# State-space loop of a two-layer trunk: gated pieces of one channel block over both pairs, decays in SBUF, two PSUM banks for input products, parameter tables loaded in two parts

## The chip, the cores and the metric

One core of a Trainium2 chip runs the whole kernel. The metric is the device time of one execution in microseconds; shown is the median of three. The engines are PE (TensorE), DVE (VectorE), ACT (ScalarE), POOL (GpSimd) and SP, which here only issues transfers.

## The reference, cut to what matters

A trunk of two layers over 256 frames of 2048 channels. Layer 0 mixes with a gated linear recurrence and windowed attention, layer 1 with a grouped state-space model (128 groups of 16 channels, 64 complex states each) and a gated layer; each layer has a squared-ReLU MLP of hidden size 8192. The change touches the mixer of layer 1:

```
h = rmsnorm(x, mix_norm_o[j])
# s5_grouped
lam_bar = exp(lam * step);  bu = einsum('blgh,gph->blgp', u, b_bar)
_, h = lax.associative_scan(_linear_combine, (broadcast(lam_bar), bu), axis=1)
y = real(einsum('blgp,ghp->blgh', h, c)) + d_skip * u
# gated layer
g = gelu(y) @ w_glu[j]
val, gate = split(g, 2, axis=-1)
x = x + val * sigmoid(gate)
```

All of it is float32. A product with a weight is done as two matmuls: the rounded weight `Wh` times the operand and its remainder side by side (512 columns), and the weight's remainder `Wl` times the operand (256 columns).

## The kernel before, in words

**Weights.** A weight matrix is taken in pairs of 128 output channels (256 columns); a pair is four units of 512 rows. SP loads a unit to `raw`, ACT rounds it to `Wh` (L1055), DVE writes the remainder `Wl = raw - Wh` (L1418), PE runs 16 matmuls for each unit. ACT (L1060) and DVE (L1489) evict a finished pair from its two PSUM banks in `ps`; the second pair behind needs these banks, so `pair` on PE waits for `pair_read` of the pair two before it.

**The state-space loop.** The 2048 channels are 16 blocks `c`. The frames are handled four at a time, so 64 steps are left to scan; four groups of steps with real and imaginary part make 512 columns. Per block:

- POOL `s5_input` (L2195): scales the input rows `us` by the norm's factor. Five are done ahead of the loop (`INPUTS_AHEAD`), then one in each step of the loop.
- PE `s5_in`: 32 matmuls of 64x64x64 with the table's rows into `v_bank`: `px[:,0]` for even blocks, `ps[:,1]` for odd ones below block `V_ALONE = 13`, `px[:,0]` for all from 13 on.
- DVE `s5_rotate` (L1792, L1793): two multiplies with the table's cos and sin, from PSUM to `ab`.
- POOL `s5_turned` (L2202): `zb`, their difference.
- ACT `s5_decay` (L1332): fills the PSUM bank `px[:,1]` with the block's decays, behind the scan before it.
- DVE `s5_scan` (L1801): `tensor_tensor_scan` over `px[:,1]` and `zb` into `px[:,3]`, then two multiplies with cos and sin to `pp` (L1806, L1807).
- POOL `s5_unturned` (L2208): adds the two parts of `pp`.
- PE `s5_out`: 48 matmuls with the table's output columns into `px[:,2]`.
- ACT `s5_gelu` (L1341) to `yb`; SP stores it to `y_d` and loads it turned to `yt` (L564); ACT `s5_high` (L1346) and POOL `s5_low` (L2213) write it to the operand `A2`.

DVE's order is rotate(c+1), scan(c), `pp`(c). PE's step c is `s5_in(c+1)`, `s5_out(c-2)`, and from c = 10 a piece of the gated layer. POOL's step c is turned(c), unturned(c-1), an input, and from c = 6 to 13 low(c-6); the lows 8 to 15 come behind the loop.

**Tables.** Each block has one of 1 MB in DRAM (`par_d`): columns `S_IN:S_OUT` are the rows for `s5_in`, then output columns, direct part, cos, sin. Six slots in SBUF hold them. SP loads table c+6 whole, once `s5_out(c)` has been done and after the store of block c; five of the six first ones are loaded during the last MLP phase of layer 0.

**The gated layer beside the loop.** Its first two pairs are eight units `u` (s, h = divmod(u, 2): quarter s of the rows, pair h). `glu_piece(n)` is one half (t) of one unit: eight matmuls, for which all four channel blocks of quarter s must be there. Pieces 0 to 5 stand in steps 10 to 15, piece 6 ahead of `s5_out(15)`, pieces 7 to 15 behind it. Piece 3 waits for the rotation of block 11, because the loop uses a bank of `ps`.

**Behind the loop.** SP loads the next pair's weights (`load_third`) behind the last turned block. ACT and DVE split two units of them, then evict pair `P_GLU`, split the third, evict the pair behind it, split the fourth. PE goes on with pair `P_GLU + 2`.

## Time and profile before

| | |
|---|---|
| median of three executions | 2044.24 us (2044.02 to 2044.94) |
| the profiled execution | 2049.94 us |
| its span | 2048.2 us |
| PE busy | 1999.4 us, 98% |
| DVE busy | 1341.9 us, 66% |
| ACT busy | 941.2 us, 46% |
| POOL busy | 710.3 us, 35% |
| mean granted TensorE clock | 0.996 |

The busy times are sums over the span, and matmuls overlap, so PE's is close to the whole. The loop with the state-space model lies between about 1068 and 1142 us. A row of a timeline has the start, the duration, the engine, the line, the operation with its output and inputs, the count, and in brackets how long the engine stood before it and what released it.

### The profile page before, as it was taken

How to read it: one execution, taken by the hardware profiler on the slowest of the kernel's cores; microseconds unless marked ns; L12 is line 12 of the kernel's file. 1: busy time of each engine (PE TensorE's matmuls, PEld its weight loads, DVE VectorE, ACT ScalarE, POOL GpSimd, SP SyncE). 2: the span in 40 equal slices, each digit the busy share in tenths (PEclk: the TensorE clock that was granted, in tenths of full speed). 3: DMA queues.
4: the chain of work that ended last, by engine and by line, in shares of the span. 5: the costliest groups of instructions: out<-in, count | busy, mean ns of one | idle time of the engine just before them, and what ended most of it. 6: DMA issues, size and time to landing. Idle time of an engine off the chain costs nothing.

```text
span 2048.2 us, 35555 instructions
## 1 busy us (share of the span) xinstructions
PE 1999.4 (98%) x12950; PEld 1723.3 (84%) x12950; DVE 1341.9 (66%) x1470; ACT 941.2 (46%) x1244; POOL 710.3 (35%) x910
## 2 busy tenths in 40 slices
PE   8989999999999999999997999999999999999998
PEld 7778888888888888888876888888888888888887
DVE  6886888755765576566669666676566556656653
ACT  6446654444444444444553444444444444444443
POOL 3582369978677777440348311000000000000000
PEclk9999999999999999999999999999999999999999
DMA  7544567666666666676887555655556555656563
GB/s 219 177 118 134 171 182 211 197 224 203 203 201 216 204 197 226 196 261 194 290 255 261 174 184 171 198 185 186 186 182 188 190 185 175 194 185 186 180 194 128
DMA packets 374595, 399.89 MB, mean 195 GB/s; under 512 B 23152, under 2 KB 367488, under 8 KB 370400
## 3 DMA queue, kind: packets, MB, share of 16 engines
q1 hardware_dynamic: 366912, 371.77, 57.9%
q0 software_dynamic: 5216, 24.52, 4.1%
q10 hardware_dynamic: 2368, 2.24, 0.3%
q8 instruction: 67, 1.10, 0.2%
q14 instruction: 32, 0.26, 0.0%
HBM read 371.87 MB, written 25.17 MB: 194 GB/s over the span
## 4 chain that ended last, share of the span: by engine, by line
PE 88%; DVE 5%; ACT 3%; POOL 2%; issue 1%; DMA 1%; ACTq 0%; DVEq 0%; POOLq 0%; SPq 0%
PE ps L654 55%; PE ps L656 27%; DVE Wl L1418 1%; PE px L877 1%; ACT Wh L1055 1%; POOL pp L2208 1%; PE ps L990 1%; POOL zb L2202 1%; PE px L839 1%; DMA raw<-in_w_up_dram 0%; ACT pb L1135 0%; PE ps L625 0%; PE ps L839 0%; PE px L790 0%; POOL us L2195 0%
## 5 line engine op out<-in xcount | busy, mean ns | idle before, releaser
L654 PE MATMUL ps<-A,Wh 128*128 128x512 f32 x5024 | 1766.1, 400 | 4.5 <-issue 2.4
L656 PE MATMUL ps<-A,Wl 128*128 128x256 f32 x5024 | 1359.5, 281 | 0.0
L1418 DVE TENSOR_TENSOR Wl<-raw,Wh 128x1024 fp32r<-128x1024 f32 x660 | 840.7, 1286 | 563.4 <-ACT Wh L1055 556.9
L654 PEld LDWEIGHTS ps<-A,Wh 128*128 128x128 f32 x5024 | 926.1, 188 | 213.8 <-issue 6.0
L1055 ACT ACTIVATE Wh<-raw 128x1024 fp32r<-128x1024 f32 x660 | 689.9, 1058 | 738.7 <-PE ps L656 463.1
L656 PEld LDWEIGHTS ps<-A,Wl 128*128 128x128 f32 x5024 | 948.4, 189 | 28.9
L1249 ACT ACTIVATE A<-cross 128x512 f32 (+1 forms) x64 | 40.5, 633 | 207.2 <-DVE cross L1737 207.2
L1903 POOL TENSOR_TENSOR sq<-xT 128x512 f32<-128x512 f32 (+1 forms) x23 | 32.2, 1399 | 285.6 <-DVE xT L1823 152.7
L1489 DVE TENSOR_TENSOR cross<-ps,cross 128x512 f32<-128x512 f32 x161 | 110.0, 683 | 16.9 <-ACT cross L1060 16.6
L1060 ACT ACTIVATE cross<-ps 128x512 f32<-128x512 f32 x163 | 94.8, 581 | 11.5 <-PE ps L654 10.0
L1740 DVE TENSOR_TENSOR A<-cross,A 128x512 f32 (+1 forms) x64 | 47.5, 743 | 57.5 <-ACT A L1249 57.5
L1499 DVE TENSOR_TENSOR xT<-xT,cross 128x512 f32<-128x512 f32 (+1 forms) x72 | 53.9, 748 | 7.2 <-DVE cross L1489 5.9
L2125 POOL TENSOR_TENSOR t<-cti,lamp 128x256 f32<-128x256 f32 x16 | 19.9, 1244 | 96.7 <-ACT cti L1287 96.7
L1737 DVE SCALAR_TENSOR_TENSOR cross<-cross 128x512 f32<-128x512 f32 x64 | 49.3, 771 | 2.2
L1735 DVE TENSOR_TENSOR cross<-cross,rs 128x512 f32<-128x512 f32 x64 | 47.4, 741 | 2.2
L1506 DVE SCALAR_TENSOR_TENSOR A<-xT,pcol,A 128x256 fp32r<-128x256 f32 (+1 forms) x32 | 30.5, 1000 | 12.1 <-ACT A L1376 11.2
L1904 POOL TENSOR_TENSOR ss<-ss,sq 128x512 f32<-128x512 f32 x23 | 33.1, 1440 | 1.8
L2030 POOL TENSOR_TENSOR stg<-t 128x32 f32<-128x32 f32 (+2 forms) x48 | 32.1, 669 | 3.8
L2028 POOL TENSOR_TENSOR t<-stg 128x32 f32<-128x32 f32 (+2 forms) x48 | 27.3, 569 | 3.8
L2026 POOL TENSOR_TENSOR t<-stg 128x32 f32<-128x32 f32 (+2 forms) x48 | 25.3, 527 | 3.8
L990 PE MATMUL ps<-A,Wh 128*128 128x512 f32 x64 | 24.1, 417 | 1.9 <-POOL A L2213 1.1
L2029 POOL TENSOR_TENSOR t<-stg 128x32 f32<-128x32 f32 (+2 forms) x48 | 24.2, 504 | 3.8
(345 smaller groups left out, 1377.8 us busy)
## 6 DMA issues: line engine op xcount, KB each, us to landing
raw<-in_w_up_dram SPq DMA_DIRECT2D x256, 512.0 KB, 4.0
raw<-in_w_down_dram SPq DMA_DIRECT2D x256, 512.0 KB, 4.1
raw<-in_w_glu_dram SPq DMA_DIRECT2D x64, 512.0 KB, 4.3
raw<-in_w_in_e_dram SPq DMA_DIRECT2D x52, 512.0 KB, 3.9
raw<-in_w_out_e_dram SPq DMA_DIRECT2D x32, 512.0 KB, 3.4
s_params<-stg POOLq DMA_DIRECT2D x16, 1024.0 KB, 5.4
slot<-s_params SPq DMA_DIRECT2D x12, 1024.0 KB, 6.6
xin<-in_x_dram SPq DMA_DIRECT2D x4, 512.0 KB, 8.0
```

The source lines that it names most:

```text
L654: wide = lambda: mm(ps[:, b + t, :], Wh[:, s, c, cols], A[:, k, :], start=(n == 0), stop=(n == KC - 1))
L656: half = lambda: mm(ps[:, b + t, 0:L], Wl[:, s, c, cols], A[:, k, 0:L], start=False, stop=False)
L990: wide = lambda: mm(ps[:, 2 * d + t, :], Wh[:, u % NU, c, cols], A2[:, k, :], start=(k == 0), stop=(k == KC - 1))
L1055: fn(Wh[:, s], raw[:, s], ACT.Copy).then_inc(hi_split, 1)
L1060: fn(cross[:, d], banks[:, :, L:2 * L], ACT.Copy).then_inc(crossed, 1)
L1249: hi.inc(fn(A2[:, bass.ds(j * 2, 2), 0:L], cross[:, c], ACT.Copy))
L1418: tt(Wl[:, s], raw[:, s], Wh[:, s].bitcast(F32), ALU.subtract).then_inc(lo_split, 1)
L1489: tt(cross[:, d] if dest is None else dest, banks[:, :, 0:L], cross[:, d], ALU.add).then_inc(pair_read, 1)
L1499: tt(xs, xs, cross[:, d], ALU.add).then_inc(x_final, 1)
L1735: link(tt(cross[:, c], cross[:, c], rs2, ALU.mult))
L1737: stt(cross[:, c], cross[:, c], 0.0, cross[:, c], ALU.max, ALU.mult).then_inc(hid_ready, 1)
L1740: tt(A2[:, k, L:2 * L], cross[:, c], A2[:, k, 0:L].bitcast(F32), ALU.subtract).then_inc(a2_ready, 1)
```

## The change

- `v_bank`: `px[:,0]` and `px[:,1]` in turn for all blocks. `V_ALONE` goes, with the waits that belonged to it.
- Decays: a new SBUF tile `decays` with two buffers takes the place of `px[:,1]`. ACT fills it one block earlier, and the scan reads it there.
- Tables: `load_rows(c)` loads `S_IN:S_OUT` (256 KB) once `s5_in(c-6)` is done, `load_rest(c)` the other 768 KB once `s5_out(c-6)` is done. `s5_in` waits for the first, `s5_rotate` for the second. In SP's step c stand the rest of c+6 and the rows of c+8.
- Inputs: six ahead of the loop, and the other ten in steps 0 to 6 by a list, with two in steps 1, 3 and 5.
- Gated pieces: `glu_piece(k)` takes one channel block k over both pairs and both halves (eight matmuls). It waits for low(k). Pieces 0 to 6 stand in steps 8 to 14, piece 7 ahead of `s5_out(15)`, pieces 8 to 15 behind it. Both units of a quarter are done in its last piece.

```diff
@@ -65,8 +65,7 @@
 NP2 = 32 + NH
-V_ALONE = 13
-INPUTS_AHEAD = 5
+INPUTS_AHEAD = 6
 P_Q = 0
@@ -182,6 +181,7 @@
             ab = sb("ab", [P, 2, 2, TPC, 2, NC4], on=o)
             zb = sb("zb", [P, 2, TPC, 2, NC4], on=o)
             pp = sb("pp", [P, 2, 2, TPC, 2, NC4 + 1], on=o)
+            decays = sb("decays", [P, 2, TPC, 2, NC4], on=o)
             yb = sb("yb", [P, 2, TPC, NC4], on=o)
             yt = sb("yt", [P, 4, L], on=o)
             uc = sb("uc", [P, 2, 2, CT, NC4], on=o)
@@ -251,7 +251,8 @@
         kd_loaded = sem("kd_loaded")
         landed = [sem(f"landed{s}") for s in range(NU)]
         bc_loaded = sem("bc_loaded")
-        slot_loaded = [sem(f"slot_loaded{s}") for s in range(NSLOT)]
+        rows_loaded = [sem(f"rows_loaded{s}") for s in range(NSLOT)]
+        rest_loaded = [sem(f"rest_loaded{s}") for s in range(NSLOT)]
         stg_stored = [sem(f"stg_stored{s}") for s in range(2)]
         kd_stored = sem("kd_stored")
         kd_shifted = sem("kd_shifted")
@@ -377,16 +378,11 @@
         def v_bank(c):
-            bank = ps[:, 1] if c % 2 and c < V_ALONE else px[:, 0]
-            return bank.rearrange("p (t k n) -> p t k n", t=TPC, k=2)
+            return px[:, c % 2, :].rearrange("p (t k n) -> p t k n", t=TPC, k=2)
         def y_bank():
             return px[:, 2, 0:L].rearrange("p (t n) -> p t n", t=TPC)
-
-        def rho_bank():
-
-            return px[:, 1, :].rearrange("p (t k n) -> p t k n", t=TPC, k=2)
         def g_bank():
@@ -437,6 +433,10 @@
         def operands_behind(j):
             return ((0, 1), (2, 3), (4, 5, 6), (7,))[j]
+
+        def inputs_beside(c):
+
+            return {0: (6,), 1: (7, 8), 2: (9,), 3: (10, 11), 4: (12,), 5: (13, 14), 6: (15,)}.get(c, ())
         def sum_bank(n):
@@ -532,17 +532,24 @@
                 load_pair(g + 8 + j, w_down[0], (QTR - 1) * D, j * TW)
             sp.wait_ge(unit_done, (g + 8) * NU)
-            def load_slot(c):
+            def load_rows(c):
+
+                if c >= NSLOT:
+                    sp.wait_ge(s5_v, c - NSLOT + 1)
+                sp.dma_start(slot_of(c)[:, S_IN:S_OUT], par_d[c][:, S_IN:S_OUT]).then_inc(rows_loaded[c % NSLOT], 16)
+
+            def load_rest(c):
                 if c >= NSLOT:
                     sp.wait_ge(s5_y, c - NSLOT + 1)
-                sp.dma_start(slot_of(c), par_d[c]).then_inc(slot_loaded[c % NSLOT], 16)
+                sp.dma_start(slot_of(c)[:, S_OUT:S_ALL], par_d[c][:, S_OUT:S_ALL]).then_inc(rest_loaded[c % NSLOT], 16)
             sp.wait_ge(kd_stored, 16)
             for j in range(2, 8):
                 load_pair(g + 8 + j, w_down[0], (QTR - 1) * D, j * TW)
                 if j - 2 < NSLOT - 1:
-                    load_slot(j - 2)
+                    load_rows(j - 2)
+                    load_rest(j - 2)
             def load_glu(u):
                 s, h = divmod(u, 2)
@@ -566,13 +573,18 @@
             for u in range(2 * NU):
                 load_glu(u)
             sp.wait_ge(rss_ready, 1)
-            load_slot(NSLOT - 1)
+            load_rows(NSLOT - 1)
+            load_rest(NSLOT - 1)
+            load_rows(NSLOT)
+            load_rows(NSLOT + 1)
             for c in range(KC):
                 sp.wait_ge(s5_ge, c + 1)
                 sp.dma_start(y_d[c].rearrange("(t q) (j n) -> (q j) t n", t=TPC, j=CT), yb[:, c % 2])\
                     .then_inc(y_stored[c % 2], 16)
                 if c + NSLOT < KC:
-                    load_slot(c + NSLOT)
+                    load_rest(c + NSLOT)
+                if c + NSLOT + 2 < KC:
+                    load_rows(c + NSLOT + 2)
                 if c >= 1:
                     load_turned(c - 1)
             load_turned(KC - 1)
@@ -925,13 +937,9 @@
             def s5_in(c):
                 pe.wait_ge(us_ready, c + 1)
-                pe.wait_ge(slot_loaded[c % NSLOT], 16 * (c // NSLOT + 1))
-                if c == 1:
-                    pe.wait_ge(pair_read, P_GLU)
-                if 2 <= c < V_ALONE:
+                pe.wait_ge(rows_loaded[c % NSLOT], 16 * (c // NSLOT + 1))
+                if c >= 2:
                     pe.wait_ge(s5_rot, c - 1)
-                if c >= V_ALONE:
-                    pe.wait_ge(s5_rot, c)
                 for t in range(TPC):
                     for k in range(2):
                         for g in range(2):
@@ -973,32 +981,30 @@
             position_sum(cross[:, (P_GLU - 1) % 2], False, True).then_inc(rms_sum, 1)
             pe.wait_ge(rms_var, 3)
-            def glu_piece(n):
-
-                u, t = divmod(n, 2)
-                s, d = glu_unit(u)
-                if n == 0:
+            def glu_piece(k):
+
+                s, c = divmod(k, UK)
+                if k == 0:
                     pe.wait_ge(pair_read, P_GLU)
-                if n == 3:
-                    pe.wait_ge(s5_rot, V_ALONE - 1)
-                if t == 0:
-                    pe.wait_ge(lo_split, P_GLU * NU + u + 1)
-                    pe.wait_ge(a2_ready, 48 + UK * (s + 1))
-                for c in range(UK):
-                    k = s * UK + c
-                    cols = slice(t * P, t * P + P)
-                    wide = lambda: mm(ps[:, 2 * d + t, :], Wh[:, u % NU, c, cols], A2[:, k, :],
-                                      start=(k == 0), stop=(k == KC - 1))
-                    half = lambda: mm(ps[:, 2 * d + t, 0:L], Wl[:, u % NU, c, cols], A2[:, k, 0:L],
-                                      start=False, stop=False)
-                    if k == KC - 1:
-                        half()
-                        last = wide()
-                    else:
-                        wide()
-                        last = half()
-                if t == 1:
-                    last.then_inc(unit_done, 1)
+                pe.wait_ge(a2_ready, 48 + k + 1)
+                for h in range(2):
+                    u, d = 2 * s + h, (P_GLU + h) % 2
+                    if c == 0:
+                        pe.wait_ge(lo_split, P_GLU * NU + u + 1)
+                    for t in range(2):
+                        cols = slice(t * P, t * P + P)
+                        wide = lambda: mm(ps[:, 2 * d + t, :], Wh[:, u % NU, c, cols], A2[:, k, :],
+                                          start=(k == 0), stop=(k == KC - 1))
+                        half = lambda: mm(ps[:, 2 * d + t, 0:L], Wl[:, u % NU, c, cols], A2[:, k, 0:L],
+                                          start=False, stop=False)
+                        if k == KC - 1:
+                            half()
+                            last = wide()
+                        else:
+                            wide()
+                            last = half()
+                    if c == UK - 1:
+                        last.then_inc(unit_done, 1)
             s5_in(0)
             s5_in(1)
@@ -1007,13 +1013,13 @@
                     s5_in(c + 1)
                 if c >= 2:
                     s5_out(c - 2)
-                if c >= 10:
-                    glu_piece(c - 10)
+                if 8 <= c < KC - 1:
+                    glu_piece(c - 8)
             s5_out(KC - 2)
-            glu_piece(6)
+            glu_piece(7)
             s5_out(KC - 1)
-            for n in range(7, 4 * NU):
-                glu_piece(n)
+            for k in range(8, KC):
+                glu_piece(k)
             phase(P_GLU + 2, 14, A2)
@@ -1325,11 +1331,11 @@
             def s5_decay(c):
-                if c == 0:
-                    fn(rho_bank()[:, :, :, 0], ones[:, 0:2 * TPC].rearrange("p (t k) -> p t k", t=TPC), ACT.Copy, scale=0.0)
+                if c < 2:
+                    fn(decays[:, c, :, :, 0], ones[:, 0:2 * TPC].rearrange("p (t k) -> p t k", t=TPC), ACT.Copy, scale=0.0)
                 else:
-                    act.wait_ge(s5_g, c)
-                fn(rho_bank()[:, :, :, 1:NC4],
+                    act.wait_ge(s5_g, c - 1)
+                fn(decays[:, c % 2, :, :, 1:NC4],
                    rho4[:, steps_of(c)].unsqueeze(2).unsqueeze(3).to_broadcast([P, TPC, 2, NC4 - 1]), ACT.Copy)\
                     .then_inc(s5_rho, 1)
@@ -1787,6 +1793,7 @@
             def s5_rotate(c):
                 dve.wait_ge(s5_v, c + 1)
+                dve.wait_ge(rest_loaded[c % NSLOT], 16 * (c // NSLOT + 1))
                 if c >= 2:
                     dve.wait_ge(s5_z, c - 1)
                 tt(ab[:, c % 2, 0], v_bank(c), cos_of(c), ALU.mult)
@@ -1798,7 +1805,7 @@
                 dve.wait_ge(s5_rho, c + 1)
                 if c >= 1:
                     dve.wait_ge(s5_p, c)
-                nc.vector.tensor_tensor_scan(px[:, 3, :], px[:, 1, :], zb[:, c % 2].rearrange("p t k n -> p (t k n)"),
+                nc.vector.tensor_tensor_scan(px[:, 3, :], decays[:, c % 2].rearrange("p t k n -> p (t k n)"), zb[:, c % 2].rearrange("p t k n -> p (t k n)"),
                                              0.0, ALU.mult, ALU.add).then_inc(s5_g, 1)
                 dve.wait_ge(s5_g, c + 1)
                 if c >= 2:
@@ -2219,8 +2226,8 @@
                 s5_turned(c)
                 if c >= 1:
                     s5_unturned(c - 1)
-                if c + INPUTS_AHEAD < KC:
-                    s5_input(c + INPUTS_AHEAD)
+                for i in inputs_beside(c):
+                    s5_input(i)
                 if 6 <= c < KC - 2:
                     s5_low(c - 6)
             s5_unturned(KC - 1)
```

## Rows read from the trace of the kernel before

**Rows 1.** The page, chain of waits by engine, whole span (share of the span).

```profile
PE 88%; DVE 5%; ACT 3%; POOL 2%; issue 1%; DMA 1%; ACTq 0%; DVEq 0%; POOLq 0%; SPq 0%
```

**Rows 2.** Windows; from:to, length, busy (count) of each engine, clock, DMA, GB/s.

```profile
1090.00:1100.00 10.00, 7.04 (x212) 6.45 (x208) 9.93 (x15) 3.93 (x9) 8.89 (x10) 1.00 0.99 353
...
1110.00:1112.60 2.60, 2.60 (x51) 2.48 (x48) 2.43 (x3) 0.00 (x0) 2.60 (x4) 0.50 0.81 326
```

**Rows 3.** Timeline of DVE in the loop, 1099 to 1104 us.

```profile
1099.58 1.22 DVE L1801 TENSOR_TENSOR_SCAN px<-px,zb 128x512 f32<-128x512 f32 x1
...
1103.23 1.22 DVE L1801 TENSOR_TENSOR_SCAN px<-px,zb 128x512 f32<-128x512 f32 x1
```

**Rows 4.** Timeline of DVE, the loop's first rotation, a late one, its end.

```profile
1070.98 0.69 DVE L1792 TENSOR_TENSOR ab<-px,slot 128x512 f32<-128x512 f32 x1 [2.92 <-PE px L940]
...
1116.01 0.69 DVE L1792 TENSOR_TENSOR ab<-px,slot 128x512 f32<-128x512 f32 x1 [1.97 <-PE px L940]
...
1134.78 0.68 DVE L1807 TENSOR_TENSOR pp<-px,slot 128x512 f32<-128x512 f32 x1
```

**Rows 5.** Timeline of SP's queue.

```profile
1099.83 0.52 SPq L539 DMA_DIRECT2D slot_over_sums<-s_params  x1
...
1144.99 2.14 SPq L557 DMA_DIRECT2D raw<-in_w_glu_dram  x4
```

**Rows 6.** Timeline of PE in the loop.

```profile
1108.11 1.98 PE L940 MATMUL ps<-us,slot_over_sums 64*64 64x64 f32 x32 [2.88 <-POOL us L2195]
...
1114.82 1.15 PE L940 MATMUL px<-us,slot 64*64 64x64 f32 x32
...
1118.90 1.15 PE L940 MATMUL px<-us,slot 64*64 64x64 f32 x32
```

**Rows 7.** Timeline of POOL in the loop.

```profile
1074.27 1.27 POOL L2202 TENSOR_TENSOR zb<-ab 128x512 f32<-128x512 f32 x1
...
1078.42 1.27 POOL L2202 TENSOR_TENSOR zb<-ab 128x512 f32<-128x512 f32 x1
...
1104.89 1.27 POOL L2202 TENSOR_TENSOR zb<-ab 128x512 f32<-128x512 f32 x1
1106.12 1.18 POOL L2208 TENSOR_TENSOR pp<-pp 128x512 f32<-128x512 f32 x1
1107.27 0.72 POOL L2195 TENSOR_TENSOR us<-us,rss 128x256 f32<-128x256 f32 x1
1107.94 0.72 POOL L2213 TENSOR_TENSOR A<-yt,A 128x256 fp32r<-128x256 f32 x1
1108.63 1.27 POOL L2202 TENSOR_TENSOR zb<-ab 128x512 f32<-128x512 f32 x1
```

**Rows 8.** Timeline of DVE behind the loop.

```profile
1135.38 3.36 DVE L1418 TENSOR_TENSOR Wl<-raw,Wh 128x1024 fp32r<-128x1024 f32 x2
...
1138.66 1.75 DVE L1418 TENSOR_TENSOR Wl<-raw,Wh 128x1024 fp32r<-128x1024 f32 x1
```

**Rows 9.** Timeline of POOL behind the loop.

```profile
1135.54 2.12 POOL L2208 TENSOR_TENSOR pp<-pp 128x512 f32<-128x512 f32 x1 [1.50 <-DVE pp L1807]
1137.62 1.71 POOL L2213 TENSOR_TENSOR A<-yt,A 128x256 fp32r<-128x256 f32 x1
```

**Rows 10.** Groups, DVE, 0:1060, then 1300:1900; busy us, mean ns, idle before.

```profile
L1418 DVE TENSOR_TENSOR Wl<-raw,Wh 128x1024 fp32r<-128x1024 f32 x343 | 455.4, 1340 | 274.4 <-ACT Wh L1055 272.8
L1489 DVE TENSOR_TENSOR cross<-ps,cross 128x512 f32<-128x512 f32 x80 | 54.6, 682 | 7.2 <-ACT cross L1060 6.9
...
L1418 DVE TENSOR_TENSOR Wl<-raw,Wh 128x1024 fp32r<-128x1024 f32 x213 | 258.1, 1224 | 193.1 <-ACT Wh L1055 189.5
```

**Rows 11.** Timeline of ACT behind the loop.

```profile
1150.91 1.06 ACT L1055 ACTIVATE Wh<-raw 128x1024 fp32r<-128x1024 f32 x1 [0.43 <-DMA raw<-in_w_glu_dram]
```

**Rows 12.** Timeline of DVE, the eviction of pair P_GLU.

```profile
1153.14 0.68 DVE L1489 TENSOR_TENSOR cross<-ps,cross 128x512 f32<-128x512 f32 x1
```

**Rows 13.** Timeline of PE, the first matmul of pair P_GLU + 2.

```profile
1153.97 0.49 PE L654 MATMUL ps<-A,Wh 128*128 128x512 f32 x1
```

## The prediction

> **What bounds the kernel now.** I read the chain of waits first: 88% of it is PE, so over nearly all of the span every microsecond in which PE idles is lost [rows 1]. The windows then say where it idles: from 1090 to 1100 us PE is busy 7.04 of 10 us, with VectorE at 9.93 and GpSimd at 8.89 [rows 2]. That is the state-space loop, in which PE has too little of its own to do and VectorE and GpSimd pass each channel block back and forth. The rest of the span, two MLPs, projections and most of the gated layer, isn't touched; the change lives between 1060 and 1170 us.
>
> VectorE's timeline gives the beat of the loop: one scan starts at 1099.58 and the next at 1103.23, 3.66 us a channel block, two rotations, scan and two `pp` multiplies back to back [rows 3]. Sixteen such blocks from the first rotation at 1070.98 would end at 1129.6 us; the last `pp` multiply really ends at 1134.78 + 0.68 = 1135.46 [rows 4]. I call this end T. Of the 5.9 us between, some 0.5 went in the second block; the other 5.3 went from 1109 on, where VectorE waits for PE, longest 1.97 us [rows 4]. Their source: the table of block 11 is asked for at 1099.83 and its first matmul starts at 1108.11, 8.3 us later [rows 5, 6]. PE had stood for 2.88 us, its granted clock was 0.50 behind that [rows 2], the 32 matmuls of `s5_in` took 1.98 us where 1.15 is usual [rows 6], and then PE with a gated piece in each block needs 1118.90 - 1114.82 = 4.08 us a block [rows 6]. It never catches up.
>
> GpSimd runs at 3.74 us a block at 1104.89 to 1108.63: zb 1.24, pp 1.15, us 0.69, low part 0.69 from start to start [rows 7]. It has nearly nothing to spare either.
>
> **The change, part by part.**
>
> *Tables in two parts, rows loaded two blocks earlier.* `s5_in` now waits for rows that are asked for eight blocks ahead and are free to load once `s5_in(c-6)` is done; the 8.3 us landing [rows 5, 6] has over 20 us. The rest (cos, sin, output columns) is asked for where the whole table was, but it is first needed by the rotation, which in step with the beat starts 14.6 us after the end of block c-6's `pp`. The way to the request (sum, `s5_out`, gelu, the store ahead of it) took 5.1 us for block 5: its `pp` ended a beat and a rotation, 4.9 us, ahead of scan 7 at 1099.58, and the request is at 1099.83 [rows 3, 5]. The landing takes at most the 8.3 of the whole table, so 1.2 us are left at the old beat and more at a longer one. The wait that goes is the one of 2.88 us [rows 6]; what is late next is treated below. SP gets 16 more issues of about 0.5 us [rows 5], one or two in a beat of 3.66 us in which it issues two or three of that length otherwise and waits for the rest: nothing. Bounds: 0 to -5.3 us.
>
> *Two banks for the products all through.* The wait of `s5_in(c)` for the rotation before it (c from 13) goes, part of the 5.3 us. The gated pieces no longer share a bank with the loop.
>
> *Gated pieces by channel block.* The matmuls are the same 128, eight to a piece. [rows 6] hold one piece beside one `s5_in` and one `s5_out` in 4.08 us. Eight instead of seven now stand ahead of `s5_out(15)`, beginning at c = 8. PE at 4.08 us against a beat of 3.66 falls behind 0.42 us a block, 7 x 0.42 = 2.9; `s5_in` is one block early and has about 2.3 us of room before VectorE notices. Price at that beat 0.3 to 0.6 us; at a beat of 4.07 (below) nothing.
>
> *Inputs earlier on GpSimd.* The same ten scalings inside the loop, but none from c = 7 on. At the old beat this would free it: 1.24 + 1.15 + 0.69 = 3.08 us a block.
>
> *Decays in SBUF.* This decides. ScalarE's fill gets two buffers and moves off the way between two scans; its engine is at 3.93 of 10 us [rows 2], so it costs nothing. But the scan, which had one operand in PSUM and one in SBUF, now has both in SBUF. Look at what an instruction of VectorE with both inputs in SBUF does beside GpSimd. The split of weights has a mean of 1224 ns where GpSimd is idle, and 1340 over the first 1060 us, where it often works; the eviction, with one input in PSUM, has 682 in the latter [rows 10]. Behind the loop both meet: the first two splits end at 1135.38 + 3.36 = 1138.74, 0.9 us late, and the third takes 1.75 us [rows 8]. GpSimd's pp add, 1.19 us elsewhere, takes 2.12, and its low part, 0.73 elsewhere, 1.71 [rows 9, 7]. Laid side by side: split to 1136.6, pp add to 1137.66, split to 1138.74, low part to 1139.33, split to 1140.41. They take turns, each stands while the other runs: 1.08 us of split after the release, 0.59 of a low part. In the loop before, all VectorE instructions have one input in PSUM, and rotations and scans keep their 0.69 and 1.22 us beside a full GpSimd [rows 3, 4, 7].
>
> The trace has no scan with two SBUF inputs beside a busy GpSimd, so bounds: 0 if it is exempt, and if not, 1.08 us of GpSimd's time for each scan. I take the second; nothing in the rows ties it to the kind of operation. The Trainium skill ("SBUF — State Buffer", section "SBUF: two separate sides") says that a VectorE instruction with two SBUF inputs and a GpSimd instruction that reads SBUF hold one pair of ports by turns, each for its full length; it excepts no operation. By that rule the sum below holds; if it did not cover the scan, rival 1 would.
>
> **The sum.** GpSimd now needs, a block, 1.24 + 1.15 + 0.69 + 1.08, less some 0.09 that the stopped instruction has already behind it: 4.07 us; with a second short operation (two inputs, or input and low part) 4.76. Both are over VectorE's 3.66, so GpSimd sets the beat. Step by step by the start of the zb subtraction: block 1 at 1074.3 as before; block 2 at 1080.3 (4.15 us before, plus one more input 0.69, the scan's hold 1.0, and 0.25 of the first scan behind an input); blocks 3 to 14 nine steps of 4.07 and three of 4.76 (c = 3, 5, 6), 50.9 us, so 1131.2. From there one pp add 1.24 + 1.2, scan 14 to 1134.7, its `pp` to 1135.9, scan 15 and its `pp`: T = 1138.5. Before it was 1135.46: +3.1 us. In this beat PE has 4.07 for its 4.08, so it neither wins nor loses.
>
> *After T nothing is given back.* PE is free sooner: one piece fewer is left behind `s5_out(15)`, and a piece starts when its own channel is there, not four. I put the end of the pieces at T + 15.5 to T + 16.5, an estimate; before, it is T + 18.5. But the next pair must wait for the eviction of `P_GLU`. That stands on VectorE behind the split of the next weights, which ScalarE gets at 1150.91 [rows 11], from loads that SP issues from 1144.99 on, behind the last turned block [rows 5]. The eviction runs from 1153.14 [rows 12], PE goes on at 1153.97, T + 18.5 [rows 13]. Neither order on SP nor on VectorE changes, so PE goes on at T + 18.5 and the freed 2 to 3 us become idle. The result is T's shift alone: +3.1, to which PE's own pauses, hidden or not, add 0 to 1; I take 3.2. The profiled execution took 2049.94 us over a span of 2048.2 and the median is 2044.24; I put the difference on the median: **2047.4 us**.
>
> **Rivals.**
> 1. *The scan isn't stopped by GpSimd.* Then VectorE keeps 3.66, the 5.3 us go, less 0.3 for PE's lag: T at 1130.5, -5.0 us, 2039.2. For it: no row has such a scan. Against: rows 8 to 10.
> 2. *Slower: PE falls to the low clock again in the slower beat.* Before c = 8 PE has some 2.5 us of work (4.08 less a piece) in 4.07 to 4.76, so it idles longer than it did. If the clock falls as the pieces begin, an `s5_in`, an `s5_out` and a piece cost PE 6.7 us, 1108.11 to 1114.82, instead of 4.08 [rows 6]: +2.6, of which the 2.3 us of room hides little if it comes twice or with a pause. About 3 us more: 2050.4. It decides where the fall meets a gated piece; earlier, twice 2.5 us of work at the low clock is 5.0 us against 4.76, which the room covers. For it: 2.88 us of idle did it once [rows 6]. Against: with PE at 7.04 of 10 us busy it stayed at 1.00 [rows 2]. The idle 2 to 3 us after the pieces may do the same to the next pair, at a like price.
> 3. *The landed rest comes late*, and the rotation waits where `s5_in` did: between 0 and 1 us a block; it would need over 9.5 us for a landing, and at a beat of 4.07 another 1.6. At 1 us a block for five blocks it would be +8, 2052.
>
> **How the numbers follow.** Exclusion as summed 0.62 (own range 2045.5 to 2049.5), rival 1 0.17, rival 2 0.19, rival 3 0.02. A measurement of this kernel tells about 0.2%, 4.1 us, from no change: the bounds are 2040.15 and 2048.33. Faster: rival 1, less a part that keeps some loss, 0.16. Slower: rival 2 and 3 and a quarter of the first, 0.35. Within: 0.49. The range for 8 in 10 reaches from 2038.9 to 2051.0.
>
> **What would show it.** Right: scans of 1.3 to 2.4 us instead of 1.22; GpSimd instructions of 128x512 at over 2 us once a block; scan to scan 4.1 and 4.8 us; GpSimd without idle time from 1078 on; no wait of `s5_in` for a table; T near 1138.5; PE idle 2 us ahead of the next pair, which starts at T + 18.5. Wrong: scans all at 1.22 and a beat of 3.66 (rival 1), a granted clock of 0.5 between 1095 and 1125 (rival 2), VectorE's rotation waiting for a DMA (rival 3), or a next pair that starts before T + 18, which would mean that the end of the loop doesn't hang on the loads.

## The result, and the profile after

The changed kernel takes 2052.7 us (median of 6 runs, 2049.18 to 2055.44) against 2045.93 for the kernel before beside it (6 runs, 2044.02 to 2047.68): ratio 1.0029 with an interval of 1.0019 to 1.004. It is slower by 0.3%. The forecast was 2047.4 with a range up to 2051.0, so the time lies above the range. The profiled execution took 2053.77 us over a span of 2051.9.

The beat of the loop came out nearly as forecast, 4.0 and 4.65 us a block for 4.07 and 4.76. This is the timeline of VectorE (DVE) after the change, in two blocks next to each other; columns as in [rows 3], which it answers:

```profile
1086.86 0.68 DVE L1799 TENSOR_TENSOR ab<-px,slot_last 128x512 f32<-128x512 f32 x1
1087.46 0.68 DVE L1800 TENSOR_TENSOR ab<-px,slot_last 128x512 f32<-128x512 f32 x1
1088.06 1.55 DVE L1808 TENSOR_TENSOR_SCAN px<-decays,zb 128x512 f32<-128x512 f32 x1
...
1092.07 2.20 DVE L1808 TENSOR_TENSOR_SCAN px<-decays,zb 128x512 f32<-128x512 f32 x1
...
1096.70 1.54 DVE L1808 TENSOR_TENSOR_SCAN px<-decays,zb 128x512 f32<-128x512 f32 x1
```

And GpSimd (POOL) beside it, which answers [rows 7]:

```profile
1086.10 1.27 POOL L2209 TENSOR_TENSOR zb<-ab 128x512 f32<-128x512 f32 x1
1087.33 1.18 POOL L2215 TENSOR_TENSOR pp<-pp 128x512 f32<-128x512 f32 x1
1088.48 2.33 POOL L2202 TENSOR_TENSOR us<-us,rss 128x256 f32<-128x256 f32 x2
1090.77 1.26 POOL L2209 TENSOR_TENSOR zb<-ab 128x512 f32<-128x512 f32 x1
1092.00 1.18 POOL L2215 TENSOR_TENSOR pp<-pp 128x512 f32<-128x512 f32 x1
1093.14 1.64 POOL L2202 TENSOR_TENSOR us<-us,rss 128x256 f32<-128x256 f32 x1
1094.74 1.27 POOL L2209 TENSOR_TENSOR zb<-ab 128x512 f32<-128x512 f32 x1
```

Read the two against each other. The scan of 1092.07 meets a pp add that began at 1092.00 and ends at 1093.18. The scan ends at 1094.27, 1.09 us behind that. The short operation behind the pp add is marked from 1093.14 to 1094.78, 1.64 us instead of 0.72, since it stands while the scan runs. At 1088.06 the same happens with a pp add that is nearly through, so the scan is late by 0.33 only. From one zb to the next GpSimd takes 4.67 us with two short operations between (1086.10 to 1090.77) and 3.97 with one (to 1094.74). The scans follow half a block later, with steps of 4.01 and 4.63; [rows 3] have 3.66. GpSimd has no idle time between 1079 and 1136 us. The window 1090 to 1100, which answers the first of [rows 2], says it in one line:

```profile
1090.00:1100.00 10.00, 6.21 (x199) 5.80 (x194) 9.93 (x13) 3.28 (x8) 10.00 (x10) 1.00 0.97 326
```

VectorE's 9.93 are the same as before, but 0.33 or 0.98 us of each scan in it is waiting; its 13 instructions were 15. No `s5_in` waits for a table any more. From 1110 to 1112.6, where the second of [rows 2] has a clock of 0.50, it is 1.00 here; it fell earlier, last at 1102 us, which is taken up below. The loop's end, which answers [rows 4] and [rows 8]:

```profile
1072.87 0.69 DVE L1799 TENSOR_TENSOR ab<-px,slot 128x512 f32<-128x512 f32 x1 [2.91 <-PE px L948]
...
1137.01 2.22 DVE L1808 TENSOR_TENSOR_SCAN px<-decays,zb 128x512 f32<-128x512 f32 x1
1139.26 0.69 DVE L1813 TENSOR_TENSOR pp<-px,slot 128x512 f32<-128x512 f32 x1
1139.87 0.68 DVE L1814 TENSOR_TENSOR pp<-px,slot 128x512 f32<-128x512 f32 x1
1140.47 5.01 DVE L1424 TENSOR_TENSOR Wl<-raw,Wh 128x1024 fp32r<-128x1024 f32 x3
```

T is 1139.87 + 0.68 = 1140.55. From the first rotation the loop takes 67.68 us, against 64.48 in [rows 4]: +3.2, where the prediction has +3.1. Its start is 1.89 us later than in the profile before; the kernel before differs from itself by as much (1070.98 and, in e1, 1073.07). And PE goes on with the next pair sooner behind T, which answers [rows 13]:

```profile
1157.74 0.49 PE L666 MATMUL ps<-A,Wh 128*128 128x512 f32 x1 [1.45 <-DVE cross L1495]
```

That is T + 17.19 instead of T + 18.51. From there to the end of the span both have the same: 894.16 and 894.23 us. So the profiled difference of 3.7 us of span is 3.2 of loop, less 1.3 behind it, and 1.9 of a later start.

By these rows the mechanism inside the loop was right. But the two kernels' medians differ by 6.8 us and the loops of the two profiles by 3.2, and that had to be settled.

### The profile page after: what moved, and what is told of

Read it like the earlier page. It is cut to its first block, busy times and chain, and to the rows that moved or that the text cites. A ratio compares the mean times of both kernels' runs of the same rounds, so it can differ in the third digit from the quotient of the medians.

```text
span 2051.9 us, 35569 instructions
## 1 busy us (share of the span) xinstructions
PE 2002.6 (98%) x12950; PEld 1727.2 (84%) x12950; DVE 1349.7 (66%) x1470; ACT 940.3 (46%) x1245; POOL 724.7 (35%) x910
## 4 chain that ended last, share of the span: by engine, by line
PE 86%; DVE 7%; ACT 3%; issue 2%; DMA 1%; POOL 0%; SPq 0%; ACTq 0%; DVEq 0%
PE ps L666 55%; PE ps L668 27%; DVE Wl L1424 1%; DVE px L1808 1%; PE px L889 1%; ACT Wh L1061 1%; DVE pp L1814 1%; PE ps L637 0%; DMA raw<-in_w_up_dram 0%; ACT pb L1141 0%; DVE ab L1800 0%; PE ps L851 0%; PE px L802 0%; DVE cross L1495 0%; PE px L872 0%
## 5 line engine op out<-in xcount | busy, mean ns | idle before, releaser
L666 PE MATMUL ps<-A,Wh 128*128 128x512 f32 x5024 | 1767.8, 400 | 5.8 <-issue 2.1
L1808 DVE TENSOR_TENSOR_SCAN px<-decays,zb 128x512 f32<-128x512 f32 x16 | 27.7, 1732 | 0.1
L1347 ACT ACTIVATE yb<-px 128x256 f32<-128x256 f32 x16 | 6.1, 384 | 45.8 <-PE px L966 45.8
L2033 POOL TENSOR_TENSOR t<-stg 128x32 f32<-128x32 f32 (+2 forms) x48 | 25.7, 536 | 3.8
L2036 POOL TENSOR_TENSOR t<-stg 128x32 f32<-128x32 f32 (+2 forms) x48 | 25.3, 526 | 3.8
```

The source lines that it names most:

```text
L666: wide = lambda: mm(ps[:, b + t, :], Wh[:, s, c, cols], A[:, k, :], start=(n == 0), stop=(n == KC - 1))
L1808: nc.vector.tensor_tensor_scan(px[:, 3, :], decays[:, c % 2].rearrange("p t k n -> p (t k n)"), zb[:, c % 2].rearrange("p t k n -> p (t k ...
```

## The experiments

The edits are shown cut to their deciding lines, with `...` for the rest of a long argument. Three lengths can be read in any run: the loop from the first rotation to T; PE's restart, which is its first matmul of pair `P_GLU + 2` counted from T, whether it stood before it or not; and the restart to the end of the span, which is 893.97 to 894.28 us in all twelve traces and is left out below.

| kernel | loop | restart | span | ratio to the kernel before |
|---|---|---|---|---|
| before, first profile | 64.48 | T + 18.51 | 2048.2 | |
| e1 before again | 59.42 | T + 18.43 | 2045.2 | |
| changed | 67.68 | T + 17.19 | 2051.9 | 1.0029 (1.0019 to 1.004) |
| e2 changed again | 68.79 | T + 17.22 | 2051.4 | 1.0022 (1.0013 to 1.0031) |
| e3 decays alone | 69.26 | T + 18.29 | 2050.4 | 1.0031 (1.002 to 1.0043) |
| e4 two-part tables alone | 60.82 | T + 18.31 | 2044.7 | 0.999 (0.9979 to 1.0) |
| e5 inputs ahead | 70.74 | T + 17.21 | 2053.6 | one run, 2055.41 us |
| e6 decays in PSUM | 59.61 | T + 17.98 | 2045.3 | 0.9998 (0.9989 to 1.0007) |
| e7 whole tables | 67.75 | T + 17.46 | 2050.2 | 1.0031 (1.002 to 1.0042) |
| e8 loads early | 67.61 | T + 19.37 | 2050.6 | 1.0044 (1.0029 to 1.0059) |
| e9 tables, loads early | 60.02 | T + 20.82 | 2047.9 | 1.001 (1.0 to 1.002) |
| e10 PSUM, loads early | 59.42 | T + 18.93 | 2042.8 | 1.0009 (1.0 to 1.0017) |

**e1, the kernel before once more**, no edit: are the pauses of [rows 4] the kernel's, or that execution's?

> The kernel before, unchanged, profiled a second time. Theory A: the pauses of the loop (table of block 11 late, then PE at the low clock) belong to the kernel; the stretch from the first rotation to the end of the last pp multiply is 64.5 us again, and the first PE wait for a table is between 1 and 3 us. Theory B: the profiled execution before was an unlucky one (it took 2049.94 us against a median of 2044.24 of its timed runs); then this stretch is 59 to 62 us here, with scan to scan at 3.66 nearly throughout, and the true price of the change is larger than the 3.8 us between the two profiled executions.

Measured: 2046.96 us, loop 59.42. Every step from scan to scan is 3.65 or 3.66 up to the last, which has no rotation in it and is 2.67 (2.68 before). The windows of e1 that answer [rows 2]:

```profile
1090.00:1100.00 10.00, 7.32 (x230) 6.86 (x226) 9.90 (x15) 3.38 (x7) 8.88 (x10) 1.00 1.04 370
1110.00:1112.60 2.60, 2.60 (x46) 2.15 (x41) 2.56 (x5) 1.40 (x3) 2.60 (x4) 1.00 1.10 410
```

The clock is 1.00 in both; it was at 0.50 from 1080 to nearly 1086, where no rotation waited. Block 11's table has the same way as in [rows 5, 6], and its first matmul comes sooner. SP and PE of e1:

```profile
1101.93 0.50 SPq L539 DMA_DIRECT2D slot_over_sums<-s_params  x1
...
1108.21 1.15 PE L940 MATMUL ps<-us,slot_over_sums 64*64 64x64 f32 x32 [0.90 <-issue]
```

6.3 us from request to first matmul instead of 8.3, and 0.90 us of idle instead of 2.88. The row of [rows 6] names GpSimd's `us` as what ended the wait, but block 11's input was done at 1096.8 us there; the one that ended at 1107.99 is block 14's, so by elimination it was the table. VectorE never notices in e1. So 5 us of the 64.48 were that one execution's: a table 2 us later and the low clock behind it. The kernel before has now been profiled twice, once with these pauses and once without. Four more profiles have the decays in PSUM (e4, e6, e9, e10) and loops of 59.4 to 60.8 us, but their tables come in two parts, so they don't tell how often the kernel before has the late table.

**e2, the changed kernel once more**, no edit, beside the others on one chip.

> The changed kernel, unchanged, timed in five rounds and profiled again. Both theories: the loop stretch is 67 to 68 us, with a scan of 1.55 or 2.2 us in each block and a beat of 4.0 and 4.65 us, as GpSimd is never idle and leaves no room for luck. Time over the kernel before: +3.8 us if theory A holds, +6 to +9 if theory B does.

Measured: 2052.06 us, 5.0 over the kernel before beside it, which is between the two theories' numbers, and a loop of 68.79, which is above both. Three late rotations waited for PE, 0.52, 0.31 and 0.94 us; the rest is the first profile again. PE with its first gated piece, the clock at that moment, and the first late rotation of e2:

```profile
1107.23 0.79 PE L996 MATMUL ps<-A,Wh 128*128 128x512 f32 x1
```

```profile
1107.00:1108.00 1.00, 1.00 (x8) 0.79 (x6) 1.00 (x3) 0.66 (x3) 1.00 (x2) 0.50 0.91 349
```

```profile
1119.82 0.69 DVE L1799 TENSOR_TENSOR ab<-px,slot 128x512 f32<-128x512 f32 x1 [0.52 <-PE px L948]
```

The low clock reached into the first piece: 2.40 us from its first matmul (1107.23) to the next `s5_in` (1109.63), where the first profile has 1.72 (1108.09 to 1109.81). The `s5_in` of block 11 then ends 0.4 us ahead of its rotation instead of 1.9, and a pause of 0.61 us in PE's issue behind it is enough to make the next rotation late.

**e3, the decays alone.** The kernel before, with only this:

```diff
+            decays = sb("decays", [P, 2, TPC, 2, NC4], on=o)
-                    act.wait_ge(s5_g, c)
-                fn(rho_bank()[:, :, :, 1:NC4],
+                    act.wait_ge(s5_g, c - 1)
+                fn(decays[:, c % 2, :, :, 1:NC4],
-                nc.vector.tensor_tensor_scan(px[:, 3, :], px[:, 1, :], zb[...],
+                nc.vector.tensor_tensor_scan(px[:, 3, :], decays[:, c % 2]..., zb[...],
```

> The kernel before with one part of the change alone: the decays in SBUF in two buffers; tables, banks, inputs and pieces as before. Theory (exclusion between the scan and GpSimd): GpSimd's beat is 4.0 us with one short operation and 4.67 with two; by steps the loop stretch is 67 us, scans take 1.55 to 2.2 us, and the time is as long as the changed kernel's, +4 to +7 us over before. Rival (the loss is in the tables or in the order of the pieces): scans 1.22 us, time within 1 us of before.

Measured: 2053.81 us, loop 69.26 for the 67 expected. It has the whole loss. VectorE, then GpSimd, of e3:

```profile
1083.10 1.54 DVE L1802 TENSOR_TENSOR_SCAN px<-decays,zb 128x512 f32<-128x512 f32 x1
1087.08 1.55 DVE L1802 TENSOR_TENSOR_SCAN px<-decays,zb 128x512 f32<-128x512 f32 x1
```

```profile
1085.13 1.27 POOL L2203 TENSOR_TENSOR zb<-ab 128x512 f32<-128x512 f32 x1
1086.36 1.18 POOL L2209 TENSOR_TENSOR pp<-pp 128x512 f32<-128x512 f32 x1
1087.51 1.64 POOL L2196 TENSOR_TENSOR us<-us,rss 128x256 f32<-128x256 f32 x1
```

The pattern is that of the changed kernel, without any other part of the change. Late in the loop three rotations also waited for PE, 0.20, 0.17 and 1.18 us; the clock was 0.50 from 1111 to 1117 us, as the first pieces began.

**e4, the tables in two parts alone.** The kernel before, with only `load_rows` and `load_rest` for `load_slot`:

```diff
+                sp.dma_start(slot_of(c)[:, S_IN:S_OUT], par_d[c][:, S_IN:S_OUT]).then_inc(rows_loaded[c % NSLOT], 16)
+                sp.dma_start(slot_of(c)[:, S_OUT:S_ALL], par_d[c][:, S_OUT:S_ALL]).then_inc(rest_loaded[c % NSLOT], 16)
+                if c + NSLOT + 2 < KC:
+                    load_rows(c + NSLOT + 2)
```

> The kernel before with another part alone: tables in two parts, the rows loaded two blocks earlier; decays in PSUM. Theory: no s5_in waits for a table, scan to scan 3.66 us until the pieces begin, scans at 1.22 us; loop stretch 60 to 62 us. The time is 3 to 4 us under before if the late table belongs to the kernel (A), and within 1 us of it if it was a matter of luck (B). Rival (splitting the loads costs: 16 more transfers, the rotation waits for the rest): rotation waits for a DMA, loop stretch above 64.5 us, slower.

Measured: 2045.7 us, ratio 0.999 with an interval up to 1.0. The scan stays at 1.22 us. The ratio stands for 2 us less and its interval for 0 to 4.3, between the two theories. The loop, 60.82 us with one wait of 1.31 us for PE, is no shorter than that of e1, so this trace shows no gain against an execution without the pause. The up to 5.3 us that the prediction allowed this part exist only against one with it; how many of the timed executions of the kernel before are of that kind no run shows.

**e5, a change of size.** All ten inputs are scaled ahead of the loop, so that GpSimd has no input beside the scans. If the scan cost more by itself from SBUF, it would be long here too.

```diff
-INPUTS_AHEAD = 6
+INPUTS_AHEAD = 16
-            return {0: (6,), 1: (7, 8), 2: (9,), 3: (10, 11), 4: (12,), 5: (13, 14), 6: (15,)}.get(c, ())
+            return ()
```

> The changed kernel with all sixteen input scalings ahead of the loop instead of six, so that GpSimd has no short operation in steps 0 to 5 and one (the low part) from 6 to 13. A size test of the theory that scan and GpSimd exclude each other: the first zb starts 10 x 0.69 = 6.9 us later; then 1.24 + 1.15 + 1.0 = 3.4 us of GpSimd's time a block is under VectorE's 3.67, so the beat is 3.7 us up to block 6 and 4.0 from there. Loop stretch about 6.9 + 64 = 71 us. Rival (a scan from SBUF costs VectorE itself 0.3 to 1 us whatever GpSimd does): beats of 4.0 or more from the start, scans of 1.5 us even beside an idle GpSimd.

Measured: one run of 2055.41 us, loop 70.74, with a wait of 6.34 us ahead of the first scan for the inputs now ahead of it. GpSimd, then VectorE, of e5:

```profile
1088.20 1.19 POOL L2215 TENSOR_TENSOR pp<-pp 128x512 f32<-128x512 f32 x1 [0.34 <-DVE pp L1814]
1089.39 2.14 POOL L2209 TENSOR_TENSOR zb<-ab 128x512 f32<-128x512 f32 x1
1091.88 1.19 POOL L2215 TENSOR_TENSOR pp<-pp 128x512 f32<-128x512 f32 x1 [0.34 <-DVE pp L1814]
```

```profile
1089.23 1.25 DVE L1808 TENSOR_TENSOR_SCAN px<-decays,zb 128x512 f32<-128x512 f32 x1
1092.91 1.24 DVE L1808 TENSOR_TENSOR_SCAN px<-decays,zb 128x512 f32<-128x512 f32 x1
...
1111.60 1.57 DVE L1808 TENSOR_TENSOR_SCAN px<-decays,zb 128x512 f32<-128x512 f32 x1
```

A scan with both inputs in SBUF takes 1.24 us if nothing stands before it. GpSimd has room here, the subtraction carries the stop (2.14 instead of 1.27) and the step is 3.68. From block 7 on the low parts fill the room, and the step is 4.0 again. So the loss is neither the scan's own duration nor the stop as such. It is the stop on an engine without slack.

**e6, the other way round.** The changed kernel with its decays back in PSUM. The products of odd blocks go to `ps[:,1]` for it, all through, the last quarter of each of the first eight gated pieces, whose bank that is, waits for the last rotation, two more low parts stand in the loop, and ScalarE's splits for the second pair move:

```diff
-                nc.vector.tensor_tensor_scan(px[:, 3, :], decays[:, c % 2]..., zb[...],
+                nc.vector.tensor_tensor_scan(px[:, 3, :], px[:, 1, :], zb[...],
-                if 8 <= c < KC - 1:
-                    glu_piece(c - 8)
+                if c >= 8:
+                    glu_piece(c - 8, ((0, 0), (0, 1), (1, 0)))
+            pe.wait_ge(s5_rot, KC)
+            for k in range(8):
+                glu_piece(k, ((1, 1),))
```

> The changed kernel with the decays back in their PSUM bank, and the products of odd blocks in ps[:,1] all through. The gated pieces in the loop take three of the four halves (six matmuls instead of eight, blocks 0 to 7); the fourth, whose bank the loop holds, follows behind the last rotation. Lows 8 and 9 are done within the loop. Tables in two parts and inputs as in the changed kernel. Theory: scans 1.22 us, beat 3.66 throughout, loop stretch 59.4 to 60.5 us; PE 3.6 us of work a block, so no wait of VectorE; the next pair starts at T + 15.5 to 17.2. Time 8 to 9 us under the changed kernel and 2 to 4 under before. Rival (the pieces by block or the tables cost the time, not the decays): loop stretch above 62, time within 3 us of the changed kernel.

Measured: 2045.72 us, 0.4 under the kernel before beside it and 6.3 under e7, which was timed with it. VectorE of e6:

```profile
1102.20 1.22 DVE L1815 TENSOR_TENSOR_SCAN px<-px,zb 128x512 f32<-128x512 f32 x1
...
1105.86 1.22 DVE L1815 TENSOR_TENSOR_SCAN px<-px,zb 128x512 f32<-128x512 f32 x1
```

The 8 us of loop are gone, which settles the cause from the other side. The hoped-for 2 to 4 us under the kernel before are not there. Of the 1.2 us that the changed kernel gains behind T, 0.8 are lost here, because PE has more left there (its pieces end at T + 17.2 instead of T + 15.7): ScalarE (ACT) waits for it at the eviction.

```profile
1149.76 0.60 ACT L1073 ACTIVATE cross<-ps 128x512 f32<-128x512 f32 x1 [1.32 <-PE ps L1000]
```

**e7, the changed kernel with whole tables**: `load_slot` and its waits as before.

```diff
-                pe.wait_ge(rows_loaded[c % NSLOT], 16 * (c // NSLOT + 1))
+                pe.wait_ge(slot_loaded[c % NSLOT], 16 * (c // NSLOT + 1))
```

> The changed kernel with the tables loaded whole again, as before; all else as changed. Theory: in the longer beat of 4.0 to 4.66 us the whole table lands in time, no s5_in stands for it longer than 0.5 us, and the time is within 1.5 us of the changed kernel. Rival (the split tables are needed once pieces stand in the loop from block 8): s5_in waits for a table by over 1 us in several blocks, time 2 to 5 us above the changed kernel.

Measured: 2051.98 us, loop 67.75, scans 1.58 and 2.20. That is the changed kernel's time. At a step of 4.0 a whole table is early enough.

**e8 to e10, the restart.** The prediction hung PE's restart on the loads of the next weights [rows 5, 11]. In the changed kernel (e8), in e4 (e9) and in e6 (e10) the first two of them are asked for ahead of the last turned blocks:

```diff
+                if c == KC - 1:
+                    load_third(0)
                 if c >= 1:
                     load_turned(c - 1)
+            load_third(1)
             load_turned(KC - 1)
-            for s in range(NU):
+            for s in range(2, NU):
                 load_third(s)
```

> The changed kernel, with two of the next pair's weight loads taken out from behind the turned blocks: the first is asked for ahead of turned block 14, the second ahead of block 15. The slots they fill are free about 5 us behind the last pp multiply (T). Theory A, the prediction's premise that the restart of PE hangs on the loads: ScalarE's first split of the next weights waits no longer for the DMA (it waited 0.43 to 0.63 us) and starts where its table load ends, the second follows back to back, and PE restarts 0.6 to 1.0 us nearer to T, at T + 16.2 to 16.6 instead of T + 17.2. Theory B, that the gated pieces set it: the splits move, but cross_terms waits for PE and the restart stays within 0.3 us of T + 17.2. The scans and the beat stay as they are (1.55 and 2.2 us; 4.0 and 4.6 us). Time: 0 to 1 us under the changed kernel, which is less than the measurement tells.

> The kernel before with its tables in two parts and the same two weight loads taken forward: decays in PSUM, pieces as before. Here cross_terms of the second bank waited 1.06 us for PE after the first had gone. Theory A (loads set the restart): restart at T + 17.3 to 17.7 instead of T + 18.3, time 0.5 to 1 us under the kernel with two-part tables alone, 1.5 to 2.5 under the kernel before. Theory B (pieces set it): restart stays at T + 18.3 and the time at that of two-part tables alone (ratio 0.999). Loop 59.4 to 61 us, scans 1.22.

> The changed kernel with its decays back in PSUM and three banks for the products, as run before, and the same two weight loads taken forward. In that kernel cross_terms waited 1.32 us for PE, so both theories expect little: restart stays at T + 17.7 to 18.0. Loop 59.4 to 61, scans 1.22, time at that of the kernel before to 1 us under it. If the restart falls by 0.6 or more, the wait for PE was not what held it.

Measured: the restart moves away from T, by 2.2 us in e8, 2.5 in e9 and 1.0 in e10; 2055.88, 2048.77 and 2048.05 us. Neither theory had the restart move away. ScalarE at the same place, in the changed kernel and then in e8:

```profile
1149.66 0.42 ACT L1352 ACTIVATE A<-yt 128x256 fp32r<-128x256 f32 x1
1150.77 0.42 ACT L1352 ACTIVATE A<-yt 128x256 fp32r<-128x256 f32 x1 [0.69 <-DMA yt<-s_y_d]
1151.20 1.28 ACT L1374 ACT_TABLE_LOAD   x1
1153.17 1.06 ACT L1061 ACTIVATE Wh<-raw 128x1024 fp32r<-128x1024 f32 x1 [0.69 <-DMA raw<-in_w_glu_dram]
```

```profile
1148.49 0.42 ACT L1355 ACTIVATE A<-yt 128x256 fp32r<-128x256 f32 x1 [2.12 <-DMA yt<-s_y_d]
1150.44 0.42 ACT L1355 ACTIVATE A<-yt 128x256 fp32r<-128x256 f32 x1 [1.53 <-DMA yt<-s_y_d]
1150.88 1.28 ACT L1377 ACT_TABLE_LOAD   x1
1152.17 2.00 ACT L1064 ACTIVATE Wh<-raw 128x1024 fp32r<-128x1024 f32 x2
```

The wait for the weights is gone in e8 and the two splits run back to back, as theory A had it. But the turned blocks, small loads asked for behind half a megabyte each, come late: block 15 at T + 13.4 instead of T + 10.2. ScalarE's order puts the table load and the splits behind them, and PE stands 2.98 us for the eviction. In e9 it is the pieces that come late: PE stands 2.29 us for the low part of a late turned block, its pieces end at T + 21.0, and the next pair follows without a pause. The restart hangs on the last turned block as much as on the weights, and moving the one forward moves the other back. So these runs don't show what the loads alone are worth.

No version is faster than the kernel before beyond its interval; e4 and e6 are level with it.

## Why the prediction was wrong

**Right.** *Decays in SBUF.* The turns of scan and GpSimd, 1.08 us per scan on GpSimd less what the stopped operation had behind it: steps of 4.0 and 4.64 for 4.07 and 4.76, GpSimd without idle time, scans of 1.55 and 2.20, loop +3.2 for +3.1 against the same execution. That the last two agree so well is partly luck. The twelve steps from the third zb to the fifteenth took 49.9 us (1082.12 to 1132.04), not 50.9; but the last scan, which the sum had at its full speed, was stopped too (2.22 us), and from the fifteenth zb to T it took 8.5 us, not 7.3. The trace agrees with the rule that the prediction took from the Trainium skill ("SBUF — State Buffer", section "SBUF: two separate sides"), by which one of the two instructions has the shared ports for its whole length and the other stands, and shows it for a scan too. e3 and e6 show that this part is the whole loss. Rival 1, a scan that isn't stopped, is refuted; e5 also refutes a scan that is slower in itself.

*Rival 2, the clock.* It came true as an event and cost nothing in the first profile. A window of the changed kernel:

```profile
1102.00:1105.00 3.00, 3.00 (x62) 3.00 (x64) 2.97 (x5) 0.41 (x2) 3.00 (x3) 0.52 0.99 361
```

PE had been busy for 0.88 of the 3 us before it, and was at its low level of 1.2 GHz for nearly all of these 3, but this is ahead of the gated pieces (the first starts at 1108.09), and no rotation waited: the prediction's point from which it decides was not reached. In e2 it was: the low clock met the first piece, and the three late waits, 1.8 us together, follow. The clock is back at 1.00 when they come, and PE, which has 4.08 us of work for a step of 4.0, also lost 0.61 and 0.39 us to pauses in the issue of matmuls; which share is the clock's no run separates. e3 has the like, 1.55 us. So in these two a part of rival 2 came true, at less than its 3 us.

*Tables and two banks.* No wait of `s5_in` for a table, rival 3 did not come. But what these parts bring was sized against a pause that one of the kernel's two profiles has.

**The step that failed: "I put the difference on the median".** The sum compared the changed loop with the loop of one execution, 64.48 us, and added the difference to a median over all. The reading of [rows 4] itself held the warning: of the 5.9 us between sixteen steps of 3.66 and the execution's T, 5.3 came from a single late table with a low clock behind it. The prediction took them as the kernel's. e1 has the same kernel without them: its loop is 5.1 us shorter. The price against such an execution is 67.7 - 59.4 = 8.3 us, not the 3.1 of the sum. The prediction's own loop, 1138.5 - 1070.98 = 67.5 us, less the 59.4 of e1 would have given 8.1 and 2052.3 us, near the measured 2052.7; part of that agreement is luck, as the next term shows. The profiled execution stood 5.7 us above the median of 2044.24; the prediction named that gap and did not ask for its cause. The pauses are as long as most of it, but no run shows what the executions at the median had. The gap alone would prove nothing either, since the loop's start also moves: it is 2.1 us later in e1 than in the first profile.

**A second term was off the other way.** *"After T nothing is given back"*: 1.2 to 1.3 us are (T + 17.2 against 18.4 and 18.5), and the prediction's own sign of being wrong, a next pair ahead of T + 18, came. It let the eviction of `P_GLU`, and by it the loads, set PE's restart in both kernels. In the kernel before PE doesn't stand there at all: [rows 13] have no wait, and the last gated piece ends just then. In the first profile the eviction was done at T + 18.4 as well, so its rows couldn't tell the two apart; e1 can. VectorE, then PE, of e1:

```profile
1149.55 0.68 DVE L1489 TENSOR_TENSOR cross<-ps,cross 128x512 f32<-128x512 f32 x1
```

```profile
1150.68 0.40 PE L990 MATMUL ps<-A,Wh 128*128 128x512 f32 x1
1150.92 0.40 PE L654 MATMUL ps<-A,Wh 128*128 128x512 f32 x1
```

The eviction is done at T + 17.7, and PE goes on at T + 18.4 straight out of its last piece. e3 and e4 have the same (17.9 and 18.3; 17.8 and 18.3). In the changed kernel the pieces end at T + 15.7, the eviction at T + 17.0, and PE stands 1.45 us for it. So the freed pieces give back what lay behind the eviction, and the eviction itself is 0.7 us sooner than in e1: block 15 is read at T + 10.2 instead of 10.7, the next weights are asked for at T + 8.5 instead of 9.0. What brings those forward is open; ScalarE's last `yb` is at T + 3.9 instead of T + 4.4, but it is so in e3 too, which reads block 15 at T + 10.9. e3, e4 and e7 (T + 17.5, pieces to T + 15.7) leave the order of the pieces, the banks and the inputs as what frees PE; the order of the pieces is the likely one, and none of the three was run alone. The forecast of what would be idle was near: 1.45 us for 2, and pieces to T + 15.7 for T + 15.5 to 16.5.

8.3 - 1.2 = 7.1 us is then the difference between an execution of each without those pauses. The medians differ by 6.8 in the first set of runs and the ratios give 4.5 (e2) to 5.9. What stays open is how often the kernel before has its pauses in runs without a profile, which could take up the rest, and why the loop's start lies between 1068.6 and 1073.6 us in the twelve traces, where even the two of the unchanged kernel before lie 2.1 us apart.

## What to carry to other kernels

Before an operand moves from PSUM to SBUF, look which engines then have all their inputs in SBUF at the same time: the cost is paid by the engine that has no slack, here GpSimd with 1 us a block, and not by the one whose operand moved. A difference worked out against one profiled execution must be freed of that execution's chance pauses first, by a count of undisturbed steps; a distance from the median is a reason to look, and a second profile of the same kernel is the cheapest check. Where an engine goes on without a pause, its own work set the time, whatever else was ready at that moment. Small loads that a long chain waits for should not be queued behind large ones, even where the large ones are also awaited.

## What the runs showed of the hardware

The two engines hand over by turns, at the end of an instruction: a scan that arrives 0.07 us after the start of a GpSimd operation of 1.18 us is marked 2.20 instead of 1.22, so it waits for nearly all of it, and the next GpSimd operation waits for nearly all of the scan (1.64 instead of 0.72), though GpSimd's queue was never empty. The waiting engine goes next. The three splits behind the loop, beside GpSimd, show the same at 1.67 us each (5.01 for three) instead of 1.23. From the request of one table to its first matmul it took 6.3 and 8.3 us in two executions of the same kernel. And with two weight loads queued ahead of it, a turned block's load took 4.95 us from request to use (1145.49 to 1150.44 in e8); in e5, without them, the same block has 2.0 us (T + 8.1 to T + 10.1).
